# Rotary halves exchanged by on-chip transfers instead of by a permutation product, in a two-block transformer kernel

## The reference

```
def apply_rope(x, cos, sin):
    x1, x2 = x[..., :d2], x[..., d2:]
    return concatenate([x1 * c - x2 * s, x1 * s + x2 * c], axis=-1)
```

## Time and profile before

| what | value |
|---|---|
| time, median of 3 runs | 1266.06 us (1260.59 to 1267.25) |
| the profiled execution's own time | 1260.99 us |
| its span | 1259.2 us |
| ACT busy | 609.6 us (48%) |
| DVE busy | 791.7 us (63%) |
| POOL busy | 66.4 us (5%) |
| q1 (SP's queue) | 208.21 MB, 53.8% of the 16 engines' span |

### The profile page before, as it was taken

How to read it: one execution, slowest core, us unless ns; L and a number is a source line. 1 busy time by engine, 2 the same in 40 slices (tenths; PEclk the granted TensorE clock), 3 DMA queues, 4 the chain that set the end, 5 groups by cost and what they waited for, 6 DMA issues and landing times. The chain is left out here.

```text
span 1259.2 us, 21554 instructions
## 1 busy us (share of the span) xinstructions
PE 1228.6 (98%) x8764; PEld 1131.6 (90%) x8764; DVE 791.7 (63%) x1095; ACT 609.6 (48%) x831; POOL 66.4 (5%) x58
## 2 busy tenths in 40 slices
PE   8999999999999999999999899999999989999997
PEld 7999999989998999999999789999999978999996
DVE  4665556657866655555799655555458977654554
ACT  5444345355536443435755554444465464544343
POOL 0000000200000000000530000000004200000000
PEclk9999999999999999999999999999999999999999
DMA  9576565455335565556465056655644734566550
GB/s 286 176 227 193 175 184 149 129 159 169 134 119 199 179 192 197 173 193 185 151 126 168 28 174 203 197 175 193 187 140 119 159 101 151 174 195 192 176 198 33
DMA packets 200915, 209.62 MB, mean 166 GB/s; under 512 B 58136, under 2 KB 177552, under 8 KB 200848
## 3 DMA queue, kind: packets, MB, share of 16 engines
q1 hardware_dynamic: 200400, 208.21, 53.8%
q10 hardware_dynamic: 448, 0.46, 0.2%
HBM read 207.61 MB, written 1.05 MB: 166 GB/s over the span
## 5 line engine op out<-in xcount | busy, mean ns | idle before, releaser
L1366 DVE TENSOR_TENSOR w_lo<-raw,w_hi 128x2048 fp32r<-128x2048 f32 (+2 forms) x192 | 432.9, 2258 | 270.5 <-ACT w_hi L1014 269.9
L1014 ACT ACTIVATE w_hi<-raw 128x2048 fp32r<-128x2048 f32 (+2 forms) x192 | 359.4, 1876 | 246.3 <-PE bank L1890 214.8
L1890 PE MATMUL bank<-n_hi,w_hi 128*128 128x256 f32 (+1 forms) x1600 | 455.4, 285 | 1.5 <-DVE w_lo L1366 1.5
L1890 PE MATMUL bank<-n_hi,w_lo 128*128 128x256 f32 (+1 forms) x1600 | 452.8, 283 | 0.0
L1890 PE MATMUL bank<-n_lo,w_hi 128*128 128x256 f32 (+1 forms) x1600 | 452.7, 283 | 0.0
L1890 PEld LDWEIGHTS bank<-n_hi,w_hi 128*128 128x128 f32 (+1 forms) x1600 | 305.3, 191 | 5.6 <-DVE w_lo L1366 1.7
L1890 PEld LDWEIGHTS bank<-n_lo,w_hi 128*128 128x128 f32 (+1 forms) x1600 | 305.3, 191 | 2.1 <-issue 0.2
L1890 PEld LDWEIGHTS bank<-n_hi,w_lo 128*128 128x128 f32 (+1 forms) x1600 | 305.3, 191 | 0.0
L1890 PE MATMUL bank<-w_hi,hid_hi 128*128 128x512 f32 x440 | 172.7, 392 | 1.3 <-DVE hid_lo L1439 1.1
L1890 PE MATMUL bank<-w_lo,hid_hi 128*128 128x512 f32 x440 | 171.8, 391 | 0.0
L1890 PE MATMUL bank<-w_hi,hid_lo 128*128 128x512 f32 x440 | 171.4, 389 | 0.0
(11 more groups left out here) (268 smaller groups left out, 1485.5 us busy)
## 6 DMA issues: line engine op xcount, KB each, us to landing
raw<-in_w_ff_dram SPq DMA_DIRECT2D x64, 1024.0 KB, 5.3
raw<-in_w_in_dram SPq DMA_DIRECT2D x31, 1024.0 KB, 5.4
raw<-in_ffn_down_dram SPq DMA_DIRECT2D x22, 1024.0 KB, 4.9
raw<-in_ffn_up_dram SPq DMA_DIRECT2D x21, 1024.0 KB, 5.4
raw<-in_ffn_gate_dram SPq DMA_DIRECT2D x20, 1024.0 KB, 5.4
raw<-in_w_out_dram SPq DMA_DIRECT2D x12, 1024.0 KB, 5.1
raw<-in_w_in_dram SPq DMA_DIRECT2D x12, 256.0 KB, 4.0
raw<-in_w_uq_dram SPq DMA_DIRECT2D x24, 128.0 KB, 4.0
```

The source lines that it names most:

```text
L1014: nc.scalar.activation(wh(s)[:, c0:n], raw[:, s % RING, c0:n], ACT.Copy).then_inc(hi_ready, 1)
L1366: V.tensor_tensor(wl(s)[:, c0:n], raw[:, s % RING, c0:n], wh(s)[:, c0:n].bitcast(f32), ALU.subtract).then_inc(lo_ready, 1)
L1890: mm = MM(out, stat(k, a), mov(k, b), start=(first and k == 0 and n == 0), stop=(last and k == K - 1 and n == 2), skip_group_check=True)
```

## The change

- The two permutation matrices and the product of each rotation go. The sine tables carry the sign instead (minus in the first half of each head).
- SP gets a new step, `swap_halves`. Ahead of a given slab's load it waits until ACT has copied the projection (the bank's release), until the previous user of the swap buffer has been summed, and issues one transfer from SBUF to SBUF for each `half` of the 128 partitions: 4 transfers of 32 partitions, or 8 of 16 for qi, ki, kr and uq, of 512 columns (256 for sk, ak, ki, 32 for kc). That slab is the fifth after the one the projection used (kc: the fifth after gate 0), and never an earlier one than the rotation's before. So in a layer of the second block qi's stand before slab ckv, those of ak and ki before slab aq, aq's before rg, rk's before uq 1, those of rq and kr before uq 2, and uq's before the first slab of the output product. In all 124 transfers.
- Three swap buffers: `swap0`, a free part of `work`, and `turn_s` (for ki and rq, with a further wait for the last output that used it).
- DVE waits for `swap_in` instead of the bank, multiplies the swap buffer in place by the signed sines, and adds.
- The rotations take no PSUM bank any more. The rotation sq1 moves behind the slab gate 0, kr behind uq 0.

```diff
-CONST1 = [("ident", 128), ("perm64", 128), ("perm32", 128), ("inv64", 1), ("blk", 8), ("fold", 32),
+CONST1 = [("ident", 128), ("inv64", 1), ("blk", 8), ("fold", 32),
...
+    def sign(half):
+
+        return np.where((np.arange(P) // half) % 2 == 0, -1.0, 1.0).astype(np.float32)[:, None]
...
-    S += scores[0] + [("proj", 0, "sq1"), ("rope", 0, "nq1"), ("cmpt", "k")] + scores[1] + [("rope", 0, "sq1")] + turned[0]
-    S += gate[0] + [("cmp2", "k")] + scores[2] + weighted[0] + turned[1]
+    S += scores[0] + [("proj", 0, "sq1"), ("rope", 0, "nq1"), ("cmpt", "k")] + scores[1] + turned[0]
+    S += gate[0] + [("rope", 0, "sq1"), ("cmp2", "k")] + scores[2] + weighted[0] + turned[1]
...
-              ("rope", l, "rk"), ("proj", l, "rv"), ("rope", l, "rq"), ("rope", l, "kr"), ("rows", l),
-              ("uq", l, 0), ("ret", l, 0), ("ret", l, 1), ("ret", l, 2), ("ret", l, 3),
+              ("rope", l, "rk"), ("proj", l, "rv"), ("rope", l, "rq"), ("rows", l),
+              ("uq", l, 0), ("rope", l, "kr"), ("ret", l, 0), ("ret", l, 1), ("ret", l, 2), ("ret", l, 3),
...
+        swap0 = sb("swap0", [P, 512])
+        swap = [swap0, wflat[:, 1536:2048], turn_s]
...
+        SWAPAT, SWAP, _landed, _user = [], {}, [0] * 3, [None] * 3
+        for u, r in RO.items():
+            came = XSC[u][0]
+            at = SL[came[:3]] + 5 if came[0] in ("proj", "uq") else SL[("gate", 0)] + 5
+            SWAPAT.append((u, max(at, SWAPAT[-1][1]) if SWAPAT else at))
+            b = r % 2 if u[0] == 0 else (r - RO[(u[0], "qi")]) % 3
+            _landed[b] += 16 * (8 if u[1] in ("qi", "ki", "kr", "uq") else 4)
+            SWAP[u] = (b, _landed[b], _user[b])
+            _user[b] = r
...
+            def swap_halves(s):
+
+                while swapped[0] < len(SWAPAT) and SWAPAT[swapped[0]][1] <= s:
+                    job, _ = SWAPAT[swapped[0]]
+                    b, _, user = SWAP[job]
+                    src, _, half, _, _ = rotation(*job)
+                    sp.wait_ge(*free_count(XSC[job][0]))
+                    if user is not None:
+                        sp.wait_ge(rope_done, user + 1)
+                    if b == 2:
+                        sp.wait_ge(*((merged, 4) if job[0] == 1 else (oc_ready, NT + job[0] - 1)))
+                    n = src.shape[1]
+                    for c in range(0, P, half):
+                        other = c ^ half
+                        sp.dma_start(swap[b][c:c + half, 0:n], src[other:other + half]).then_inc(swap_in[b], 16)
+                    swapped[0] += 1
+
             while s < NSLAB:
+                swap_halves(s)
...
-                    pb = await_bank(dve, st)
+                    b, landed, _ = SWAP[st[1:]]
+                    there = swap[b]
+                    dve.wait_ge(swap_in[b], landed)
...
-                    take_turn()
-                    V.tensor_tensor(view[0], view[1], s_, ALU.mult).then_inc(freed(st), 1)
-                    dve.wait_ge(*free_count(st))
+                    link(V.tensor_tensor(view[0], view[0], s_, ALU.mult))
                     dve.wait_ge(turnc_ready, r + 1)
...
-                        V.tensor_tensor(dst, view[2], view[0], ALU.add).then_inc(rope_done, 1)
-                    turn_used[0] = (rope_done, r + 1)
+                        V.tensor_tensor(dst, view[1], view[0], ALU.add).then_inc(rope_done, 1)
+                        if b == 2:
+                            turn_used[0] = (rope_done, r + 1)
...
-                elif kind == "rope":
-                    src, n, nrow, perm, _, _ = rotation(*st[1:])
-                    pe.wait_ge(*free_count(XSC[st[1:]][0]))
-                    pb = take(pe, st)
-                    if st[2] == "kc":
-                        mm = MM(pb[:, 0:32], perm, xs1[:, 0, 0:32], start=True, stop=True)
-                    else:
-                        mm = MM(pb[0:nrow, 0:n * T], perm, src, start=True, stop=True)
-                    mm.then_inc(filled(st), 1)
```

More of the change, by code:

```diff
@@ L99, in constants @@
     rows = np.arange(P)
-    put("inv64", inv(32)[rows % 32][:, None])
+    put("inv64", sign(32) * inv(32)[rows % 32][:, None])
     put("blk", (rows[:, None] // CP == np.arange(8)[None, :]).astype(np.float32))
@@ L111, in constants @@
     put("cos_a", np.cos(angles(32, rows)))
-    put("sin_a", np.sin(angles(32, rows)))
+    put("sin_a", sign(32) * np.sin(angles(32, rows)))
     put("cos_i", np.cos(angles(16, rows)))
-    put("sin_i", np.sin(angles(16, rows)))
+    put("sin_i", sign(16) * np.sin(angles(16, rows)))
     gamma = np.log1p(-np.exp2(-5.0 - np.arange(4)))
@@ L374, in two_blocks @@
         turnc_ready, rope_done = sem("turnc_ready"), sem("rope_done")
+        swap_in = [sem(f"swap_in{i}") for i in range(3)]
         sink_seen, exp_done, pv_done, o_free = sem("sink_seen"), sem("exp_done"), sem("pv_done"), sem("o_free")
@@ L417, in job @@
         def job(key, b=None, freed_by=None, of_slab=False):
-            if b is None and idle[0] and key[0] in ("rope", "toks", "rank", "rows"):
+            if b is None and idle[0] and key[0] in ("toks", "rank", "rows"):
                 b = _small[0] % 4
@@ L542, in two_blocks @@
                 RO[st[1:]] = len(RO)
-                job(st)
             elif kind == "cmp1":
@@ L698, in rotation @@
             buf = XSC[(l, "k" if name == "kk" else name)][1]
-            src = xs1 if buf == 2 else xs[:, buf, :].rearrange("p (a t) -> p a t", a=2)
-            c64, c32 = tab[l]["64"], tab[l].get("32")
+            c64, c32, flat = tab[l]["64"], tab[l].get("32"), xs[:, min(buf, 1), :]
             if name == "kc":
                 c64 = (cos_p[:, :], sin_p[:, :])
[L703 to L711, removed]
+            one, row = xs1[:, 0, :], flat if buf != 2 else None
+            pick = {"sk": (one, 1, 32, c64, skT), "kc": (one[:, 0:32], 1, 32, c64, kcR), "k": (row, 2, 32, c64, kT),
+                    "nq0": (row, 2, 32, c64, nqT[:, 0:2]), "nq1": (row, 2, 32, c64, nqT[:, 2:4]),
+                    "sq0": (row, 2, 32, c64, sqT[:, 0:2]), "sq1": (row, 2, 32, c64, sqT[:, 2:4]),
+                    "ak": (flat[:, 0:T], 1, 32, c64, akT), "ki": (flat[:, T:2 * T], 1, 16, c32, kiT),
+                    "qi": (row, 2, 16, c32, qiT), "aq": (row, 2, 32, c64, aqT),
+                    "rk": (row, 2, 32, c64, rkT), "rq": (row, 2, 32, c64, rqT),
+                    "kr": (krx.rearrange("p a t -> p (a t)"), 2, 16, c32, krR), "uq": (row, 2, 16, (con("cos_i"), con("sin_i")), qR)}
+            return pick[name]
         def operands(l, a, t, h):
@@ L982, in _ @@
                     r = RO[st[1:]]
-                    src, n, nrow, _, (cos, _), dst = rotation(*st[1:])
+                    src, n, _, (cos, _), dst = rotation(*st[1:])
                     pool.wait_ge(*free_count(XSC[st[1:]][0]))
```

25 lines of the change are left out of this document (8 added, 17 removed).

## The result

| kernel | median of the timed runs | profiled execution | its span | mean granted clock in it |
|---|---|---|---|---|
| before | 1265.08 us (1260.59 to 1267.25, 6 runs) | 1260.99 us | 1259.2 us | 0.997 |
| changed | 1273.31 us (1271.52 to 1276.55, 6 runs) | 1272.48 us | 1270.6 us | 0.990 |

The ratio is 1.0078, 95% interval 1.0055 to 1.0101: slower by 8.2 us between the medians and by 9.9 us by the ratio, past the 0.5% that count as a difference here. The forecast was 1267.0 with "slower" at 0.25, its range 1258.5 to 1279. Three of the timed executions in the tables of this document (one of e12, two of the kernel before beside e9 to e12) took 230 us or more longer than all others and are left out of every figure.

A forecast was written before the change was run, and what follows sets the result against it. It took TensorE and DVE, full side by side, as the bound, so most of the 17.0 us of removed products buys waits; -0.4 + 0.2 + 1.0 - 1.1 + 0.5 + 0.8 = +1.0 us: 1267, range 1258.5 to 1279.

The forecast's parts named there:

- the first case alone: Whole kernel: the main forecast of 1267 us, given 60%, with its own range of 1260.5 to 1274.
- The third rival: Whole kernel: the two-input lock does not act and the clock stays up, -1.6 us, 1264.5; chance 15%.
- The first rival: Whole kernel: TensorE is the bound after all, all 17.0 us of products go, 1249; chance 7%.
- First block up to the compression product: Before L2160: DVE's multiply of k, held beside POOL, starts at 245.73; +0.2 us in place of -0.7.
- The clock in the first block: Before L2160: TensorE stands 3 us and may then run at 1.2 GHz; +1.0 us (0 to +1.7).
- Slab aq: Second block, layer 1: twelve transfers of ak and ki delay this slab's load; +0.4 us (0 to +2.0).
- The second rival: SP's queue decides: 0.8 us per transfer issue delays slab aq and rq's halves; +11.4 us, 1277; chance 18%.
- Late halves of rk, rq, kr: Second block before rg, both layers: rq's halves land after DVE wants them, kr's in time; +1.3 us (0 to +3.0).
- uq 2, ukv and the output slab: Second block: these loads come 3 to 7 us later, covered by top-k work and 16 us of TensorE work.
- The lock: DVE multiplies with two SBUF inputs are held beside POOL: +0.2 us in the first block, part of +1.3 in the second.
- The term for layer 2 alone: Before layer 2's index scores: one multiply from SBUF may fall before POOL's table products; +0.7 us (0 to +0.7).
- uq's product, -0.86 a layer: Second block at 679 us, where DVE waits for TensorE: removing this product saves 0.86 us in each layer.

The follow-up runs named there:

- e12: e5 with 10 more small products of zeros before the transposes of the second block (L2233): 1264.3 us, ratio to before 1.0003.
- e9: The kernel before with POOL's cosine product left out of every rotation: 1262.9 us, ratio to before 0.9995.
- e8: e1 with POOL's cosine product left out of every rotation too: 1253.5 us, ratio to before 0.9922.
- e5: e3 with TensorE's stands filled with small products of zeros: 1267.7 us, ratio to before 1.0036.
- e6: e1 with TensorE's stands filled with small products of zeros: 1262.5 us, ratio to before 0.9984.
- e3: The changed kernel with slab aq and the first output slab loaded ahead of the transfers of ak, ki and uq: 1271.9 us, ratio to before 1.0072.
- e1: The changed kernel without its 124 transfers, DVE multiplying the projected copy (exchange of halves left out): 1268.6 us, ratio to before 1.0040.
- e7: The kernel before with 10 small products of zeros ahead of the wait for nq1's rotation: 1260.8 us, ratio to before 0.9983.
- e11: e7 with 10 more small products of zeros before the transposes of the second block (L2220): 1259.0 us, ratio to before 0.9957.
- e4: The changed kernel with all 124 transfers issued by POOL ahead of its cosine multiply: 1287.6 us, ratio to before 1.0191.
- e10: e1 with the rotation of kr back in its old place, ahead of rows and uq 0: 1269.9 us, ratio to before 1.0041.

## Why the prediction was right or wrong

The measured 1273.3 lies in the range, 0.7 us inside the top of the first case alone (1274), and 6 us above the centre. The direction came out as forecast, the size did not, and three of the prediction's own signs went against it: slab aq was split at 626.69 ("wrong" from 626 on), "rg" came 5.1 us after 666.2 in place of at most 3, and DVE, which waited for halves, was busy 37.1 of the 42 us up to its L1839 (628.5 to 670.5) in place of over 39. The other signs held: stands of 3.13 us before the compression product and of 1.31 and 2.75 before the index scores, index scores within 0.2 us of before in layer 1, and no wait for halves over 1.50 us. The third rival (no lock, clock up) is out, since both the holds and the half-clock stretches are there.

**What bounds.** Right: DVE and TensorE side by side, so that the 17.0 us of products bought nothing (with POOL's products gone as well they are worth 9, e8 against e9). The first rival (1249) needed rotations that end earlier; e8 has them, and 1253.5.

**Start of the kernel.** Predicted -0.4, measured -0.5.

**First block up to the compression product.** +0.2 predicted, +0.2 measured (247.88 against 248.15, less the start's -0.5). The multiply of k did not start late, as written, but at 244.24, and ran 1.76 us; the rotation ended at 246.7, where the forecast comes to 247.1. So the figure is right partly by luck. That is how a hold shows in these rows: as duration, not as a wait. The Trainium skill ("SBUF — State Buffer", section "Who interferes with whom") states that the two engines lock each other out when DVE has two SBUF inputs and GpSimd reads SBUF; the trace agrees, with 1.76 and 1.79 us where the multiply from a bank took 0.692 at most.

**The clock in the first block.** A stand of 3.13 us, a half-clock stretch behind it, L2173 at 3.09 us in place of 1.93: as forecast (+1.0 for 1.2). The first block as a whole came out at +0.1 where -0.3 was the sum.

**The clock in the second block: the step that failed.** I priced a lower clock at one stand only. The same reasoning (less work for TensorE means longer stands) held at "rg", the retention and the attention: four stretches there where the profile before had none, and filling them is worth 4 to 6 us (e5, e6). I also read the cost of the clock from one execution with 0.997 while the median run of before has 0.993; the change takes it to 0.989, about 4 x 1.2 = 5 us by the slope above, an estimate. The stands that decide need not be new ones: the 2.46 us at L2220 had no stretch in the profile before and had one in layer 1 of the changed kernel, after 2.18 us.

**Slab aq.** +0.4 predicted with 2.0 as its upper end; +2.6 measured. The mechanism was right, an issue was mis-sized: 0.51 us was read from three pieces of uq 0; a transfer of 16 or 32 rows took 0.59 us in the median and 0.63 from one to the next, 0.67 over these twelve, and the load then took 5.5 to land. The second rival put the point at which the queue decides at 0.6 us, and it is past that; its own 0.8 was about as far off on the other side. At "rg" the late slab was worth 2.2 us: that product comes 80.5 us after the layer's start in the changed kernel, 78.3 in e3.

**Late halves of rk, rq, kr.** +1.3 predicted (0 to 3.0); DVE waits 2.5 us for them in each layer. I had kr's halves in time; they were 0.47 late in layer 1. At "rg" of layer 1 they are worth less than the wait, 1.2 us (78.3 in e3 against 77.1 in e1): where the halves come late, the multiply of rq takes 0.69 us (in e3 from 661.80, POOL's product ends at 661.84); where nothing is waited for (e1) it is held beside it and takes 1.79.

**uq 2, ukv and the output slab.** Written off as covered by the top-k work. DVE did wait 2.87 us for the output slab, since uq's eight transfers stood before its load (0.22 in e3). But the wait was nearly covered: from "rg" to the stand at 701.10 the changed kernel takes 29.79 us, with one half-clock stretch in it, and e1, without any transfer and with one stretch as well, 29.62.

**The lock.** Priced in the first block, and in the second only as a part of the +1.3. In e1, where no transfer is late, "rg" of layer 1 still comes 1.6 us later than before. With the 1.2 of the late halves and the 2.2 of slab aq that makes the 5.0 us at "rg". The term for layer 2 alone, +0.7, came out: its index scores come 33.13 us after the layer's start in place of 32.62, in e1 33.34.

**uq's product, -0.86 a layer.** Right, but hidden by the clock. From "rg" to the first stand in the attention of layer 1 the kernel before takes 28.96 us, e5, e6 and e8, with no stretch there, 28.1 to 28.2, and the changed kernel, with one, 29.79.

Together: predicted +1.0; the profiled executions differ by 11.5, the medians by 8. By e1, the transfers are 4.7 us (1.0078 against 1.0040). The rest is a change without transfers that still is 0.4% slower. With its stands filled (e6) it comes to 0.9984 of before, at the edge of what can be told from no change, and no lower than the kernel before with one kind of stand filled (e7, 0.9983, timed beside it).

## What to carry to other kernels

Where two engines are full side by side, work taken from one can be worth nothing until the other is relieved too, as here; test both cuts and the two together before building either. Price what the freed engine does with its time: here TensorE often paid for a stand with half its clock afterwards, and a few dead products in the stand were worth 4 to 6 us. Compare the granted clock of the profiled execution with that of the timed runs before taking it for typical, and count transfers, not bytes, in a queue that also loads the weights.

## What the runs showed of the hardware that was not expected

- The spread of the kernel before, 1258.5 to 1269.8 us, follows the mean granted clock, 0.998 to 0.990. Filling two kinds of stands cut the spread to 2.6 us (e11), from 8.9 in the runs of before beside it.
- The same stand of 2.46 to 2.50 us at L2220 was followed by a half-clock stretch in some places and by none in others, within one execution too (e3: none in layer 1, one in layer 2).
- A transfer between partitions costs the issuing engine much the same for 16 rows of 1 KB as for 32 of 2 KB: 0.59 us on SP in the median, 0.50 and 0.48 on POOL, where the next product starts only behind the issues (e4, 614.76).
- An operation of DVE that POOL holds up lasts longer in these rows (1.76 us from 244.24, 1.79 from 659.80, where 0.69 is usual), rather than starting later, and taking one operation out of its way moved the hold to the next (e10).
